# Two transformer blocks on one core: the second block's projection, attention and merge in one woven stage

## The reference

```
proj = x @ w_in            # -> z, xbc, dt_raw, dq, dk, dv, dg, cq, cg, gl
# state-space branch, 32 heads of 64, state 128, both directions
xbc  = silu(centred_dwconv(xbc, width 5))          # -> xs (2048), B (4 x 128), C (4 x 128)
dt   = softplus(dt_raw + dt_bias);  a = -exp(a_log) * dt
y    = ssd(xs*dt, a, B, C) + flip(ssd(flipped...)) + d_skip * xs
y_ssd = rmsnorm(y * silu(z))
# ssd, chunks of 128 tokens: y_diag = (C B^T * exp(segment sums)) @ xs
#   states carried from chunk to chunk; y_off = C @ state * exp(a_cum)
# differential attention, 8 heads of 2 x 64
q, k = rope(dq), rope(dk)
w    = softmax(q0 k0^T / 8) - lam * softmax(q1 k1^T / 8)
y_diff = rmsnorm(w @ dv) * (1 - lambda_init) * silu(dg)
# attention to 256 memory tokens, 4 heads of 256
y_cross = softmax(cq mk^T / 16) @ mv * silu(cg)
gates  = sigmoid(gl + gate_b)                       # 3 x 1024
merged = gates0*(y_ssd @ w_br_ssd) + gates1*(y_diff @ w_br_diff) + gates2*(y_cross @ w_br_cross)
x = layernorm(alpha * x + merged @ w_out)
```

## Time and profile before

| | |
|---|---|
| median of 3 runs | 4894.24 us (4889.57 to 4907.12) |
| profiled execution | 4892.64 us, span 4890.9 us |
| PE, DVE, ACT busy | 4204.4, 2676.2, 1640.2 us |
| mean granted clock of PE | 0.913 |
| second block, layer 0 | about 2147 to 3517 us of the span |
| second block, layer 1 | about 3517 to 4891 us |

### The profile page before, as it was taken

The page is one execution under the profiler, slowest core; times in us unless marked ns, Lnnn a source line. Parts: engine busy times, 40 slices in busy tenths (PEclk is TensorE's granted clock), DMA queues, the critical chain, the costliest instruction groups (busy, mean ns, idle before and its releaser), DMA issues.

```text
span 4890.9 us, 52047 instructions
## 1 busy us (share of the span) xinstructions
PE 4204.4 (86%) x20660; PEld 3414.6 (70%) x20660; DVE 2676.2 (55%) x4196; ACT 1640.2 (34%) x2808; POOL 125.7 (3%) x235
## 2 busy tenths in 40 slices
PE   1877879987888879989999987979699999779877
PEld 1766857866657768868888665657588887557666
DVE  5656535554656342356645743675566457535655
ACT  2334232223434232333344131443233442214432
POOL 0000000000000000000000000000000000000000
PEclk9978969998969799999999988999899999989988
DMA  4411025542202023224322231122333222212133
GB/s 151 145 41 65 31 69 181 184 140 82 66 1 95 31 82 95 91 94 131 101 74 67 82 108 56 62 85 91 110 110 121 69 67 93 99 52 65 48 108 112
DMA packets 219477, 434.71 MB, mean 89 GB/s; under 512 B 16913, under 2 KB 62001, under 8 KB 216161
## 3 DMA queue, kind: packets, MB, share of 16 engines
q1 hardware_dynamic: 197536, 335.12, 21.9%
q0 software_dynamic: 21696, 96.26, 5.5%
HBM read 387.27 MB, written 44.06 MB: 88 GB/s over the span
## 4 chain that ended last, share of the span: by engine, by line
PE 46%; DVE 14%; ACT 3%; issue 2%; DMA 1%; DVEq 0%; POOL 0%; ACTq 0%; POOLq 0%
PE ps L553 37%; PE ps L103 4%; DVE arena L120 4%; DVE spl L120 3%; ACT arena L191 2%; PE ps L1997 2%; PE ps L109 2%; DVE sm L141 2%; DVE arena L135 1%; DVE arena L127 1%; PE ps L1993 1%; DVE X L120 1%; ACT sph L191 1%; DVE HF L120 0%; DMA arena<-zd 0%
## 5 line engine op out<-in xcount | busy, mean ns | idle before, releaser
L120 DVE TENSOR_TENSOR spl<-ring,sph 128x1024 fp32r<-128x1024 f32 (+3 forms) x556 | 651.0, 1179 | 979.1 <-ACT sph L191 977.8
L191 ACT ACTIVATE sph<-ring 128x1024 fp32r<-128x1024 f32 (+3 forms) x556 | 561.9, 1022 | 1171.7 <-PE ps L553 781.5
L553 PE MATMUL ps<-sph,HTh 128*128 128x512 f32 (+3 forms) x1728 | 688.7, 399 | 12.7 <-ACT sm L191 5.2
L553 PE MATMUL ps<-sph,HTl 128*128 128x512 f32 (+3 forms) x1728 | 651.4, 377 | 0.0
L553 PE MATMUL ps<-spl,HTh 128*128 128x512 f32 (+3 forms) x1728 | 650.4, 376 | 0.0
L103 PE MATMUL ps<-arena 128*128 128x64 f32 (+9 forms) x2424 | 524.6, 388 | 125.2 <-DVE arena L168 55.5
L191 ACT ACTIVATE arena<-ps 128x512 f32<-128x512 f32 (+2 forms) x554 | 306.4, 562 | 907.5 <-PE ps L553 416.2
L553 PE MATMUL ps<-HTh,sph 128*128 128x512 f32 x1376 | 549.0, 399 | 58.6 <-DVE spl L120 30.1
L553 PE MATMUL ps<-sph 128*128 128x512 f32 (+1 forms) x1376 | 532.0, 387 | 63.1 <-DVE spl L120 62.9
L553 PE MATMUL ps<-HTl,sph 128*128 128x512 f32 x1376 | 542.3, 394 | 0.0
L553 PE MATMUL ps<-HTh,spl 128*128 128x512 f32 x1376 | 541.7, 394 | 0.0
(11 more groups left out here) (180 smaller groups left out, 5078.6 us busy)
## 6 DMA issues: line engine op xcount, KB each, us to landing
ring<-in_w_in SPq DMA_DIRECT2D x264, 512.0 KB, 3.8
ring<-in_ada_w SPq DMA_DIRECT2D x96, 512.0 KB, 4.4
ring<-in_w_down SPq DMA_DIRECT2D x44, 512.0 KB, 3.3
ring<-in_w_gate SPq DMA_DIRECT2D x40, 512.0 KB, 3.9
ring<-in_w_up SPq DMA_DIRECT2D x40, 512.0 KB, 4.6
ring<-in_w_mem SPq DMA_DIRECT2D x32, 512.0 KB, 3.4
ring<-in_w_out SPq DMA_DIRECT2D x32, 512.0 KB, 3.8
ring<-in_w_br_ssd SPq DMA_DIRECT2D x32, 512.0 KB, 3.8
```

Source lines behind the costliest of these rows:

```text
L120: self.e.tensor_tensor(o, a, b, op).then_inc(*self.done.up())
L191: self.e.activation(o, a, f, **kw).then_inc(*self.done.up())
L553: ins = pe.e.matmul(o, l, r, start=k0 == 0 and i == 0 and not b.pairs, stop=k0 + b.ks == b.kt and i == 3 * b.ks - 1 and (c0 > 0 or not b.p ...
```

## The change

- `proj`, `attn` and `merge` become one group and one weave, without the barriers between them; the order of blocks is dtb, then x and gl in turn (the B and C columns first), dg, cg, z, dq, dk, dq, dk, cq, dv, br 0, br 1, br 2.
- `ssd` runs by groups of eight heads, and may start when the group's columns are through the convolution. The state passes are a side job of their own, `pass`, by pairs of groups, both directions in turn; `yo` is scaled in its bank instead of in SBUF.
- silu(z) is applied to y tile by tile, from `z_ev`; it no longer goes through DRAM. It uses the Silu table instead of tanh and two DVE operations.
- dq and dk are read out by ACT into `RW`; the rotation is a DVE step of `turns`.
- `diff` takes four heads at a time (the first half, then the second); DVE weights unit n-1 after the maxima of unit n; PE transposes three units behind. `dnorm` and its loads run by halves.
- Pools: `seg` has two banks, `yd` one; convolution transposes, scores and the first 16 passes share bank 7 (`last`); the later passes and `turns` have banks 4 and 5 (`low`), `gated` 6 and 7 (`high`).
- The planner's cost of a read-out is given by each block (`cost_ev`), and counts in the first tile-step too; this also shifts side steps in the two mixer stages of the first block.

The diff, cut to its core (hunks of renamed keys, slices and loads left out):

```diff
-        POOLS = dict(gemm=(0, 1, 2, 3), side=(4, 5, 6, 7), main=(0, 1), gdn=(2, 3), att=(4, 5), hgrn=(6, 7), xm=(2,), seg=(4, 5, 6), yd=(7,),
+        POOLS = dict(gemm=(0, 1, 2, 3), side=(4, 5, 6, 7), main=(0, 1), gdn=(2, 3), att=(4, 5), hgrn=(6, 7), xm=(2,),
+                     seg=(4, 5), yd=(6,), low=(4, 5), high=(6, 7), last=(7,),
                      inv=(3, 4, 5), state=(2, 3, 4, 5))
...
-                    yield (load_d if m == 0 else 0.7 * (k0 + b.ks == b.kt), load_d if m == 0 else 0)
+                    d, a = b.cost_ev if k0 + b.ks == b.kt else (0, 0)
+                    yield (load_d * (m == 0) + d, load_d * (m == 0) + a)
...
+            def z_ev(g):
+                def act(a, m, p):
+                    n = 4 * g + m
+                    a.wait_ge(at["yz", l, n - 3] if n > 2 else at["stg", l, (39, 37, 38)[n]])
+                    t = at["zs", l, n] = a.act(STG[:, n % 3, :], p, ACT.Silu, par=True)
+                    return t
+                def dve(v, m, p):
+                    n = 4 * g + m
+                    v.wait_ge(at["zs", l, n])
+                    at["yz", l, n] = v.tt(Y[:, g, m, :], Y[:, g, m, :], STG[:, n % 3, :], ALU.mult)
+            def raw_act(n0):
+                def ev(a, m, p):
+                    n = n0 + m
+                    a.wait_ge(at["rot", l, n - 4] if n > 3 else at["yz", l, 15])
+                    t = at["raw", l, n] = a.cp(RW[:, n % 4, :], p, par=True)
+                    return t
...
-                    bank = take(pe, ("xt", l, i))
+                    bank = take(pe, ("xt", l, i), "last")
...
-        SSD = [(n // 8, n // 2 % 4, n % 2) for n in range(32)]
-        PASS = [(d, ci, m, g) for d in range(2) for ci, m in enumerate(range(4) if d == 0 else range(3, -1, -1))
-                for g in range(4)]
+        PASS = [(d, ci, ci if d == 0 else 3 - ci, g) for gp in (0, 2) for ci in range(4) for d in range(2) for g in (gp, gp + 1)]
...
+        def pass_pool(n):
+            return "last" if n < 16 else "low"
+        def pass_pe(pe, l):
+            for n in range(33):
+                if n < 32:
+                    yield (0.7, 0)
+                if n:
+                    d, ci, m, g = PASS[n - 1]
+                    if ci:
+                        bank = take(pe, ("yo", l, n - 1), pass_pool(n - 1))
+                        pe.wait_ge(at["sto", l, d, ci - 1, g])
+                        at["yo", l, n - 1] = pe.mm(bank[:, :], [(CTt[:, g, m * 128:(m + 1) * 128], STt[:, 2 * d + g % 2, :])])
+                        yield (1.4, 0)
+                    if ci < 3:
+                        bank = take(pe, ("su", l, n - 1), pass_pool(n - 1))
+                        pe.wait_ge(at["xw", l, n - 1], at["xt", l, 4])
+                        at["su", l, n - 1] = pe.mm(bank[:, :], [(BTK[:, m, g * 128:(g + 1) * 128], XW[(n - 1) % 2])])
+                        yield (1.4, 0)
...
-                        at["free", ("yo", l, n - 1)] = v.tt(r3(TB), r3(bank_of["yo", l, n - 1]), bc(NC[:, m, hh], 2, 64), ALU.mult)
-                        v.tt(yg, yg, TB, ALU.add)
+                        v.tt(r3(bank), r3(bank), bc(NC[:, m, hh], 2, 64), ALU.mult)
+                        at["free", ("yo", l, n - 1)] = at["passed", l] = v.tt(yg, yg, bank[:, :], ALU.add)
...
             def pool_before(p):
+                if which == 1:
+                    p.wait_ge(at[("br", l, 0), "merged", 7], at[(("br", l, 0), 1), 3], *[at["stg", l, 32 + j] for j in range(8)])
+                    at["cgin", l] = p.move(ld["cg"], OC, Cg.rearrange("m p n -> p m n"))
...
-        UN = [(h, m) for h in range(8) for m in range(4)]
+        UN = [(4 * nb + h, m) for nb in range(2) for m in range(4) for h in range(4)]
...
-                    s = su_d[:, n % 4, :]
-                    v.wait_ge(at["dexp", l, n])
-                    v.rec(s, s)
+                if 1 <= n < 33:
+                    i, s = (n - 1) % 3, su_d[:, (n - 1) % 4, :]
+                    v.wait_ge(at["dexp", l, n - 1])
+                    v.rec(s, s, par=True)
...
-            group(("proj", l), chunks(proj_blocks(l)), 3)
-            group(("attn", l), chunks(attn_blocks(l)))
-            b1, b2 = merge_blocks(l)
-            group(("merge", l), chunks(b1 + b2))
+            group(("proj", l), chunks(proj_blocks(l) + sum(branches(l), [])), 3)
...
-            weave(q, k, main(q, k), proj_sides(q, l), proj_gates(l))
-            if q.name not in ("pool", "sp"):
-                meet(q, key + (2,))
...
+            weave(q, k, main(q, k), second_sides(q, l), second_gates(l))
```

More of the change, by code:

```diff
@@ L401, in step, with met @@
                 due[name] = max(load["dve"] if d else q.t, load["act"] if a else q.t) + 0.3
+            def met(cond):
+                if isinstance(cond, tuple):
+                    return cond[0] in over or count.get(cond[0], 0) >= cond[1]
+                return slot >= cond
             def can():
-                return [(due.get(n, 0), n) for n, _, after, first in sides if n not in over and slot >= (
-                    first[count.get(n, 0)] if isinstance(first, dict) and count.get(n, 0) in first else
-                    0 if isinstance(first, dict) else first) and all(x in over for x in after)]
+                out = []
+                for n, _, after, first in sides:
+                    if n not in over and all(x in over for x in after):
+                        c = first.get(count.get(n, 0), 0) if isinstance(first, dict) else first
+                        if all(met(x) for x in (c if isinstance(c, list) else [c])):
+                            out.append((due.get(n, 0), n))
+                return out
             while "main" not in over:
@@ L1899, in proj_blocks @@
-            for nb in range(4):
-                out.append(Block(("z", l, nb), W, nb * 512, 512, 8, HT, stores(Zd, nb * 512, "silu", n), ready=HTR))
+            def z_ev(g):
[8 more added lines that the diff above has]
+                    at["yz", l, n] = v.tt(Y[:, g, m, :], Y[:, g, m, :], STG[:, n % 3, :], ALU.mult)
+                    return None
+                return dict(act=act, dve=dve)
@@ new lines, in dnorm_pe @@
+        def dnorm_pe(pe, l):
+            for nb in range(2):
+                yield (0, 2.6)
+                yield (3.2, 2.6)
+                yield (6, 0)
+                for k in (4 * nb, 4 * nb + 2):
+                    for kk in (k, k + 1):
+                        bank = take(pe, ("ydt", l, kk))
+                        pe.wait_ge(at["odn", l, nb])
+                        for m in range(4):
+                            at["yd_t", l, kk] = pe.tr(bank[:, m * 128:(m + 1) * 128], OD[:, m, kk * 128:(kk + 1) * 128], ident)
+                    yield (0, 1.4)
@@ new lines, in second_gates, with gate @@
+        def second_gates(l):
+            k, out = ("proj", l), {}
+            s = lambda *key: slot_after(k, key)
+            def gate(slot, name, n):
+                out.setdefault(slot, []).append((name, n))
+            for n in range(NCV, 24):
+                gate(s("x", l, ORD[n] // 4) - 4 + n % 4, f"conv{(n - NCV) % 2}", 5 * ((n - NCV) // 2) + 3)
+            gate(s("z", l, 0) - 4, "pass", pass_steps(16))
+            gate(s("z", l, 2) - 4, "pass", 999)
+            for n in range(4, 16):
+                gate(s(("dq", "dk")[n // 4 % 2], l, n // 8) - 4 + n % 4, "turns", 2 * (n - 4) + 1)
+            b0 = s("dv", l, 1)
+            gate(b0 - 4, "gated", 99)
+            gate(b0, "turns", 99)
+            b1, b2 = slot_after(k, (("br", l, 0), 1)), slot_after(k, (("br", l, 1), 1))
+            gate(b1 - 4, "dnorm", 5)
+            gate(b1 + 4, "dnorm", 99)
+            gate(b2 - 4, "cross_t", 99)
+            return out
```

601 lines of the change are left out of this document (292 added, 309 removed).

## The result

The changed kernel took 4703.69 us (median of 4 runs, 4701.66 to 4705.53), the kernel before 4897.17 us beside it (4889.57 to 4907.12): a ratio of 0.9604, 95% interval 0.9585 to 0.9622. The forecast was 4719, the range 4640 to 4850.

What follows compares the result with a forecast made beforehand. TensorE was taken as the bound, through its idle time and lower clock. Per layer -55 - 27 - 9 - 16 + 8 + 12 = -87, for both -174, from 4892.6 to 4719 us; range 4640 to 4850.

Steps and rivals of the forecast that it cites:

- The rotation: Queries and keys: copying out first, rotating later frees transposes from waiting for VectorE; gain 55 us per layer, bounds 40, 58.
- The boundary and the passes: Old stage boundary: no barriers, state passes among blocks, z tile by tile; gain 27 us per layer, bounds 15, 29.
- Attention: Difference attention by halves, one unit deeper: VectorE weights the previous unit meanwhile; gain 9 of 19 us idle per layer.
- Norm and memory attention: Second half's norm behind memory attention's scores and read-outs, some waiting for transfers; gain 16 us per layer, leaving 10.
- Conv transposes on bank 7: Convolution: 9 of 20 transpose groups wait for ScalarE's copy on the single bank; cost 8 us per layer, bounds 0, 26.
- The first sixteen passes on bank 7: State passes 0 to 15: 24 products wait 0.5 us each for VectorE on the bank; cost 12 us per layer.
- ACT table loads: ScalarE: 3 more table loads per layer at 1.283 us, 4 us on an engine at 34%; cost nothing.
- The first block: Its two mixers, reordered by new eviction costs: same work in nearly the same order; 0, allowance 10 us either way.
- A: Rival for the whole kernel: all idle and clock gains won, nothing paid; 4629 us, chance 0.17.
- B: Rival: half given back through passes on one bank, crowded z blocks, convolution; 4811 us, chance 0.2 for 4770 to 4868.
- D: Rival: norm only moves, kv and cross gate come late, TensorE stands as long; 4771 us, partly within the forecast's 0.5.
- C: Rival: each of 48 takings of bank 7 per layer stalls TensorE; slower from 2.2 us each, 4957 at 2.9; chance 0.07.

Runs made afterwards that it cites:

- the fence: Changed kernel with splits no longer made ahead over the start of the first query block; 4712.14 us, ratio 0.9627 to the kernel before.
- four pairs: New against old mixer plan in the kernel before, the changed kernel, its rerun, and with convolution transposes apart; new plan slower by 10, 22, 24 and 14 us.
- the first pair: The changed kernel and the kernel before, measured beside each other; 4703.69 and 4897.17 us, ratio 0.9604.
- both edits: Changed kernel with the first block's mixers planned by old costs and the second convolution job's transposes one slot later; 4671.65 us, ratio 0.9550.

## Why the prediction was right

- **The rotation** (-55): right in mechanism and size. -55 by the account, +50 to 55 when undone. The transposes wait 4.4 us instead of 38.0, against the "under 5" asked for. The 4 us that would be added by the table of the Trainium skill (VectorE: DVE Perf Modes, "The TRN2 errata"), an estimate from its figures, did not come: the same 64 multiplications took 421 ns out of SBUF and 416 out of the bank.
- **The boundary and the passes** (-27): -22, of which 4 to 8 are shown by the fence and the rest by the account alone. What I left at 2 us is 6.9, mainly the 6.6 us in which the gated transposes wait for y times silu(z) tile by tile.
- **Attention** (-9 of 19): mis-sized, the term is -22 and undoing the depth alone costs 23 to 28. I counted the 19 idle microseconds as the most to be had and took half off for the half norm. But the chain of one unit accounts for all of it, since taking the depth back costs more than the term; the twelve added operations of VectorE fit in (144.5 of 182 us busy). The clock of 0.97 was part of it too.
- **Norm and memory attention** (-16, leaving 10): 17 are left, 11 idle and 6 of clock, so -9. The 11 idle are what I left, but not for the reason given: nothing waited for kv or the cross gate (VectorE waited 2.9 us for one branch gate, no more for a DMA), and the 11 are eleven short waits within the softmax and its transposes. That the clock is 0.92 there was not counted as staying. Neither the halves of the norm nor the memory attention beside it was tried by itself.
- **Conv transposes on bank 7** (+8): 8.9 us of waits, 7.5 to 9.6 when removed, of which about 5 reach the end of the layer (5.6 in layer 1; 3.0 in layer 0, which is within its spread). Beside it stand 4.4 us in which products of the decay steps wait for ScalarE, which no term had.
- **The first sixteen passes on bank 7** (+12): mis-sized, at most about 2 us: 1.2 in the waits view, and two products late by 0.4 each. 24 products at 0.5 each took one tile-step between them as the rule, where mostly a decay step lay there as well. The price is right for the second half, which I didn't charge, and the changed kernel avoids it there by using two banks.
- **ACT table loads** (0): nothing on PE names one.
- **The dtb block** (not seen, -7): before it ran at a clock of 0.72 (2434 to 2471); now it stands first, where the clock is low in any case. The prediction took the first 43 us of a layer as unchanged, although the order of blocks was changed in it. This term is read from the account, and was not tried by itself.
- **The first block** (0, allowance 10 either way): this step failed. "The same work in nearly the same order" cost 10 to 24 us in four pairs, and 21 in the profiles of the first pair. The order of 42 and 44 of some 260 steps was enough for that. In the 100 us shown of the first mixer the clock is 0.67 with the new plan and 0.70 with the old one; that an added wait comes with some clock there is likely, and not shown.

That the sum came within 15 us (4719 against 4703.69) is in part luck: -87 per layer stands against -107 and -105, and 0 against +21 in the first block, and these errors partly cancel. With the mixers planned as before, the kernel takes 4681.48 us, 38 below the forecast. Of the signs that were named, the clock (0.98 to 1.00 from the first x block to the branches) and the transposes' wait of under 5 us (4.4) came; a gap of over 3 us was to be found once (3.7 us in the convolution), and the 12 us of state products on VectorE were 1.2. The rivals: neither A (4629) nor B (4811) nor D (4771) came; C's stall did appear in small when asked for, 0.4 us per product and not 2.2.

## What to carry to other kernels

A read-out that does arithmetic between a product and its transposes costs more than its own time: copying the tile out with the idle engine and doing the arithmetic some steps later gave back 51 us in 328, a third of it as clock, where the 16 tiles' arithmetic itself is some 40 us of VectorE. A bank shared between side jobs cost nothing while its release time was shorter than what stands between two takings, and must be priced by that distance. A planner's cost that is changed for one stage is to be kept from the others, or every stage that reads it has to be looked at.

## What the runs showed of the hardware that was not expected

- A matmul that waits some tenths of a microsecond for its bank hardly shows as waiting: 464 matmuls took 8.8 us longer, of which the waits view names 2.3, while 12 late products of 0.4 us each make 4.8. Compare stretches of equal counts by length.
- The same code in the same place differed by 10 us between profiled executions: the second mixer of the changed kernel took 578.3 us once and 567.9 the next time, while the medians of the two sets agree within 3 us. The kernel with both edits has the mixers in the order of the kernel before, and its first mixer ends at 666.2 us, where the three others with that order end at 656.2 to 658.1. A difference of 10 us in one profile's first block is therefore no sign of the code.
